# Hybrid decoder layer on one core: the attention sums are added tile by tile, and four other pieces of the order are moved

## The chip, the cores and the metric

The kernel runs on one core of a Trainium2 chip. Its time is the device time of one execution in microseconds (us), the median of several runs. TensorE (PE in the profile; PEld is its loading of weights) multiplies matrices, VectorE (DVE), ScalarE (ACT) and GpSimd (POOL) do the rest, and SyncE (SP) issues the DMA transfers. Each engine works through its own list of instructions in order and waits on semaphores that others count up.

## The reference, cut to what matters

The input x has 256 tokens of 2048 features, in float32.

```python
n = rmsnorm(h, attn_norm_w);  proj = n @ w_in            # 2048 -> 3376 columns
y_mla = mla_attention(...)                                # 8 heads of 128
y_nsa = nsa_attention(...)                                # 16 heads of 64, three branches, gated
y = concatenate([rmsnorm(y_mla, mla_out_norm_w), rmsnorm(y_nsa, nsa_out_norm_w)])
h = h + y @ w_o                                           # 2048 x 2048
n = rmsnorm(h, mlp_norm_w)
h = h + square(relu(n @ w_up)) @ w_down                   # 2048 -> 8192 -> 2048
return rmsnorm(h, final_norm_w)
```

## The kernel before, in words

The 256 tokens are two tiles of 128 (t = 0, 1). Each float32 product is made of three products in the type fp32r: the operand is split into a high part (`w_hi`, a copy by ScalarE) and a low part (`w_lo`, the difference, by VectorE), and TensorE multiplies high by high, high by low and low by high (L1266, L1267, L1270). All weights come as chunks of 1 MB at most, numbered c, through four buffers `raw` and two pairs `w_hi`, `w_lo`. So a chunk c can be split only when TensorE is done with chunk c - 2 (`w_used`), and TensorE starts it when `lo_done` has counted it.

Chunks 0 to 32 are the input projection, the MLA up projections and the compression weights. Chunk 22 is the first of the queries' weights; before it stand the copy of the values from PSUM (`v_sb`, L950, two tiles), the copy of the doubled keys (`k2h`, `k2l`) and chunk 21.

Chunks 33 to 48 are the output projection `y @ w_o`. Chunks 33 to 40 take the MLA half of y, 41 to 48 the NSA half, and in each half four chunks make the left 1024 output columns and four the right. A chunk has two blocks of 128 rows of weights and two tiles of tokens: four quarters of six matmuls with 512 columns. The sums of a group of four chunks stand in PSUM banks 0 and 1 (tile 0) and 2 and 3 (tile 1). After a group VectorE adds them, times the row factor `rm` or `rn` of that RMS norm, to the residual `h_sb` (`add_attention`, L1035, one instruction of 1024 columns for each tile), and the next group can't write the banks before.

A list, `PLAN`, written once and read by PE, ACT and DVE, sets the order up to chunk 44. In the output projection each quarter (`"q"`) is followed by one step (`"s"`) of attention: score, softmax, transposition and product with the values, spread over five steps (LAG = 3). `"hi"` and `"lo"` are the halves of the split of the next chunk. Step 51 finishes the last head, whose parts `yT` (L674, L832) chunk 44 needs; `"norm_n"` then sums the squares of the NSA half over the features (L1436). The root of the mean is taken by a guess from the bits on VectorE (`guess`, L851 and L852) and three rounds of Newton on GpSimd (`root_of_sums`, `improve`, L435 to L438).

Chunks 45 to 48 have no steps beside them. During them `h_sb` is turned (PE transposes, L1632, four 128-column blocks after chunk 46 and four after chunk 47) and copied out with the next norm's weights, split into high and low `xT` (`turned_hi`, L725, and `turned_lo`, L832). From chunk 49 on follows the MLP: the up projection of the first group (49 to 56), and a loop. `acc`, to which the down projection is added, is cleared by GpSimd (L518).

## Time and profile before

| | |
|---|---|
| median of 3 runs | 1080.29 us (1079.82 to 1081.09) |
| the profiled execution | 1080.06 us, of which 1078.0 us are its span |
| PE busy | 1058.9 us, 98% of the span |
| DVE, ACT, POOL busy | 634.5, 500.1, 101.7 us |
| granted clock of TensorE, mean | 0.998 |
| share of PE in the chain that ended last | 92% |

An engine's busy time is the time in which at least one of its instructions runs. Matmuls overlap, and their ends are modelled, so two matmuls' durations can't be summed. In a row of the timeline the first number is the start in us from the span's start, the second the duration of the row's instructions together, and square brackets give the idle time before them and who ended it.

### The profile page before, as it was taken

How to read it: one execution, taken by the hardware profiler on the slowest of the kernel's cores; microseconds unless marked ns; L12 is line 12 of the kernel's file. 1: busy time of each engine (PE TensorE's matmuls, PEld its weight loads, DVE VectorE, ACT ScalarE, POOL GpSimd, SP SyncE). 2: the span in 40 equal slices, each digit the busy share in tenths (PEclk: the TensorE clock that was granted, in tenths of full speed). 3: DMA queues.
4: the chain of work that ended last, by engine and by line, in shares of the span. 5: the costliest groups of instructions: out<-in, count | busy, mean ns of one | idle time of the engine just before them, and what ended most of it. 6: DMA issues, size and time to landing. Idle time of an engine off the chain costs nothing.

```text
span 1078.0 us, 14561 instructions
## 1 busy us (share of the span) xinstructions
PE 1058.9 (98%) x5706; PEld 906.8 (84%) x5706; DVE 634.5 (59%) x795; ACT 500.1 (46%) x620; POOL 101.7 (9%) x163
## 2 busy tenths in 40 slices
PE   8999999999999999999999999999999999999996
PEld 7889898888877888888888888888888888888885
DVE  4655765788765645556556545555655545655565
ACT  4646644776664544334334333433433433443434
POOL 2145100532203000000000000000000000000003
PEclk9999999999999999999999999999999999999999
DMA  9586562252335465655666656566666655656552
GB/s 332 165 209 198 180 211 85 73 196 78 94 103 157 157 195 179 191 182 192 192 195 195 188 187 186 183 192 192 195 194 189 189 183 185 191 192 195 194 196 78
DMA packets 89138, 190.44 MB, mean 177 GB/s; under 512 B 8758, under 2 KB 29836, under 8 KB 88716
## 3 DMA queue, kind: packets, MB, share of 16 engines
q1 hardware_dynamic: 88668, 189.41, 55.3%
q10 hardware_dynamic: 432, 0.52, 0.2%
q8 instruction: 24, 0.39, 0.1%
q14 instruction: 14, 0.11, 0.0%
HBM read 187.82 MB, written 2.10 MB: 176 GB/s over the span
## 4 chain that ended last, share of the span: by engine, by line
PE 92%; DVE 3%; ACT 2%; issue 1%; POOL 1%; DMA 0%; DVEq 0%; ACTq 0%
PE ps L1660 22%; PE ps L1266 14%; PE ps L1267 14%; PE ps L1270 14%; PE ps L1663 11%; PE ps L1533 2%; PE ps L1534 1%; PE ps L1537 1%; PE ps L1517 1%; PE ps L1492 1%; DVE w_lo L831 1%; PE ps L1331 1%; PE ps L1471 1%; PE ps L1518 1%; ACT w_hi L559 1%
## 5 line engine op out<-in xcount | busy, mean ns | idle before, releaser
L831 DVE TENSOR_TENSOR w_lo<-raw,w_hi 128x2048 fp32r<-128x2048 f32 (+4 forms) x198 | 402.6, 2036 | 354.7 <-ACT w_hi L566 287.8
L566 ACT ACTIVATE w_hi<-raw 128x2048 fp32r<-128x2048 f32 x119 | 228.1, 1917 | 396.3 <-PE ps L1270 200.8
L1660 PE MATMUL ps<-xT,w_hi 128*128 128x512 f32 x1024 | 279.5, 394 | 1.3 <-DVE h_sb L1035 1.0
L1660 PEld LDWEIGHTS ps<-xT,w_hi 128*128 128x128 f32 x1024 | 175.9, 189 | 26.1 <-issue 1.3
L1663 PEld LDWEIGHTS ps<-xT,w_lo 128*128 128x128 f32 x1024 | 157.1, 189 | 21.7
L1266 PE MATMUL ps<-w_hi,hidT 128*128 128x512 f32 x448 | 174.5, 390 | 0.0
L1267 PE MATMUL ps<-w_lo,hidT 128*128 128x512 f32 x448 | 174.4, 389 | 0.0
L1663 PE MATMUL ps<-xT,w_lo 128*128 128x256 f32 x1024 | 162.8, 281 | 0.0
L1270 PE MATMUL ps<-w_hi,hidT 128*128 128x512 f32 x448 | 138.1, 389 | 0.0
L559 ACT ACTIVATE w_hi<-raw 128x1024 fp32r<-128x1024 f32 (+3 forms) x75 | 103.8, 1391 | 72.0 <-PE ps L1270 41.4
L1270 PEld LDWEIGHTS ps<-w_hi,hidT 128*128 128x128 f32 x448 | 84.1, 188 | 17.6
L1267 PEld LDWEIGHTS ps<-w_lo,hidT 128*128 128x128 f32 x448 | 84.1, 188 | 17.2
L1266 PEld LDWEIGHTS ps<-w_hi,hidT 128*128 128x128 f32 x448 | 84.1, 188 | 17.1
L523 POOL TENSOR_TENSOR h_sb<-h_sb,fw 128x1024 f32<-128x1024 f32 x2 | 6.2, 3112 | 721.7 <-ACT sink L784 721.7
L1266 PE MATMUL ps<-w_hi,yT 128*128 128x512 f32 x128 | 54.4, 425 | 2.3 <-DVE h_sb L1035 2.3
L1267 PE MATMUL ps<-w_lo,yT 128*128 128x512 f32 x128 | 50.2, 392 | 0.0
L1266 PE MATMUL ps<-w_hi,xT 128*128 128x512 f32 x112 | 39.9, 356 | 0.4 <-DVE wcols L900 0.4
L1270 PE MATMUL ps<-w_hi,yT 128*128 128x512 f32 x128 | 39.8, 392 | 0.0
L1533 PE MATMUL ps<-xT,w_hi 128*128 128x256 f32 x128 | 37.1, 290 | 1.7 <-DVE w_lo L831 1.7
L1267 PE MATMUL ps<-w_lo,xT 128*128 128x512 f32 x112 | 37.9, 348 | 0.0
L662 ACT ACTIVATE probT<-ps 128x384 f32<-128x384 f32 (+1 forms) x48 | 22.2, 462 | 31.6 <-PE ps L1492 26.6
L1534 PE MATMUL ps<-xT,w_hi 128*128 128x256 f32 x128 | 36.2, 283 | 0.0
(309 smaller groups left out, 1309.1 us busy)
## 6 DMA issues: line engine op xcount, KB each, us to landing
raw<-in_w_up SPq DMA_DIRECT2D x64, 1024.0 KB, 5.3
raw<-in_w_down SPq DMA_DIRECT2D x64, 1024.0 KB, 5.5
raw<-in_w_o SPq DMA_DIRECT2D x16, 1024.0 KB, 5.6
raw<-in_w_in SPq DMA_DIRECT2D x8, 1024.0 KB, 5.2
raw<-in_w_in SPq DMA_DIRECT2D x8, 816.0 KB, 4.4
raw<-in_w_in SPq DMA_DIRECT2D x6, 832.0 KB, 8.2
raw<-in_mla_w_uq SPq DMA_DIRECT2D x12, 256.0 KB, 4.2
raw<-in_mla_w_ukv SPq DMA_DIRECT2D x4, 512.0 KB, 5.4
```

The lines of the kernel that those rows point to most:

```text
L559: act.activation(w_hi[:, split_slot(c), w0:w1], raw[:, raw_slot(c), w0:w1], ACT.Copy)\
L566: act.activation(w_hi[:, j % SPLIT, :], raw[:, j % RAW, :], ACT.Copy).then_inc(hi_done, 1)
L662: act.activation(probT[0:r, j % 2, 0:w], bank(6, w, 0, r), ACT.Copy).then_inc(pt_out, 1)
L831: return dve.tensor_tensor(dst, src, high.bitcast(F32), ALU.subtract)
L1266: pe.matmul(o, stationary(0, b, t), w_hi[:, slot, w], start=first, stop=False)
L1267: pe.matmul(o, stationary(0, b, t), w_lo[:, slot, w], start=False, stop=False)
L1270: m = pe.matmul(o, stationary(1, b, t), w_hi[:, slot, b * width + n0:b * width + n1], start=False, stop=last)
L1331: m = pe.matmul(flat[:, LOW[t] + n0:LOW[t] + n1], of_x(part, 2 * c + b, t), w_part[:, split_slot(c), CW * b + n0:CW * b + n1], start=c == ...
L1533: pe.matmul(o, w_hi[:, s, w], xT[:, 0, k, :], start=k == 0 and f == 0, stop=False)
L1534: m = pe.matmul(o, w_hi[:, s, w], xT[:, 1, k, :], start=False, stop=False)
L1660: pe.matmul(both, w_hi[:, slot, 512 * b + P * f:512 * b + P * f + P], xT[:, :, k0 + b, :], start=start and b == 0, stop=False)
L1663: m = pe.matmul(ps[:, b0 + f, 0:T], w_lo[:, slot, 512 * b + P * f:512 * b + P * f + P], xT[:, 0, k0 + b, :], start=False, stop=stop and b ...
```

## The change

Six edits, all of order or place, apart from the way the root for the NSA half is taken:

1. VectorE copies the 70 columns of `wcols` before it splits chunk 8, not after.
2. The second tile of the value copy (`v_sb`) moves behind the low halves of chunk 22, and the first low half of chunk 22 before the low part of the keys.
3. In the output projection the quarters go tile by tile: block 0 and block 1 of tile 0, then of tile 1. The add of a group is two entries, `("a", (n, t))`: tile 0 after the third quarter of the group's last chunk, tile 1 after the fourth. The attention steps that stood between groups now take the places behind quarters, so from chunk 37 each comes one quarter later than before, and from chunk 41 two. Chunks 45 to 48 are tile by tile as well.
4. The root for the NSA half: ScalarE loads the table of Sqrt and takes the root in `"norm_n"`, VectorE inverts it and does one round of Newton. GpSimd does nothing there. The table load that stood after chunk 49's split is gone.
5. The turned copies of blocks 4 to 7 stand after the split of chunk 49, behind the last group's add of tile 0. The transposes stay where they were.
6. `acc` is cleared once chunk 52 is split, not once the last head's low part is written.

```diff
-PLAN = [("hi", (CMP[0] + 1, 0)), ("k", "keys"), ("lo", (CMP[0] + 1, 0)), ("hi", (CMP[0] + 1, 1)), ("k", "rotary"), ("lo", (CMP[0] + 1, 1))]
+PLAN = [("hi", (CMP[0] + 1, 0)), ("lo", (CMP[0] + 1, 0)), ("k", "keys"), ("hi", (CMP[0] + 1, 1)), ("k", "rotary"), ("lo", (CMP[0] + 1, 1)),
+        ("k", "values")]
...
+ORDER = (((0, "hi", 0), (1, "lo", 0), (1, "hi", 1), (2, "lo", 1)), ((0, "hi", 0), (0, "lo", 0), (1, "hi", 1), (2, "lo", 1)))
 for _c in range(WO_M, WO_N + 4):
-    if _c in (WO_M + 4, WO_N):
-        PLAN += [("k", "add")] + _step(_s)
+    for _n, _part in enumerate((0, 2, 1, 3)):
+        PLAN += [("q", (_c, _part))]
+        if _n == 2 and (_c - WO_M) % 4 == 3:
+            PLAN += [("a", ((_c - WO_M) // 4, 0))]
+        PLAN += [(part, (_c + 1, half)) for at, part, half in ORDER[_c == WO_N + 3] if at == _n]
+        PLAN += _step(_s)
+        if _n == 3 and (_c - WO_M) % 4 == 3:
+            PLAN += [("a", ((_c - WO_M) // 4, 1))]
         _s += 1
...
+LATE = {WO_N + 5: TURNS[0], MLP0 - 1: TURNS[1]}
...
-            root_of_sums(1, rn[:, :])
-            pool.wait_ge(y_lo, 16)
+            pool.wait_ge(lo_done, MLP0 + 4)
             pool.memset(acc[:, :, :], 0.0).then_inc(acc0, 1)
...
+                elif i == "norm_n":
+                    act.activation(rc[:, 3:4], ones[:, :], ACT.Sqrt).then_inc(sqrt_table, 1)
+                    act.wait_ge(ysum_ok, 2)
+                    act.activation(rn[:, :], ssq[:, 8:10], ACT.Sqrt).then_inc(root_n, 1)
...
-            split_lo(8)
             dve.wait_ge(prm_t, 2)
             dve.tensor_copy(wcols[:, KT:NPRM], bank(4, NPRM - KT)).then_inc(wcols_ok, 1)
             dve.wait_ge(wcols_ok, 2)
+            split_lo(8)
...
-            for t in range(TT):
-                dve.tensor_copy(v_sb[:, t, :], flat[:, 2048 + 1024 * t:3072 + 1024 * t]).then_inc(v_out, 1)
+            dve.tensor_copy(v_sb[:, 0, :], flat[:, 2048:3072]).then_inc(v_out, 1)
...
-                guess(dst, square).then_inc(guessed, 1)
+                if part == 0:
+                    guess(dst, square).then_inc(guessed, 1)
+                    return
+                y, w, minus = dst, root_w[:, 0:TT], root_w[:, TT:2 * TT]
+                link(dve.tensor_scalar(minus, square, -0.5, None, ALU.mult))
+                dve.wait_ge(root_n, 1)
+                link(dve.reciprocal(y, y))
+                link(dve.tensor_tensor(w, y, y, ALU.mult))
+                link(dve.tensor_tensor(w, w, minus, ALU.mult))
+                dve.scalar_tensor_tensor(out=y, in0=w, scalar=1.5, in1=y, op0=ALU.add, op1=ALU.mult).then_inc(yr_ok, 1)
...
             for c in range(WO_N + 4, MLP0):
-                if c == WO_N + 4:
-                    add_attention(1, 0, 5, WO_N + 3)
                 split_lo(c + 1)
-                if WO_N + 5 <= c < MLP0 - 1:
-                    for k in TURNS[c - WO_N - 5]:
-                        turned_lo(k)
-            add_attention(1, 1, 6, MLP0 - 1)
+                if c == MLP0 - 1:
+                    add_attention(1, 1, 0, 6, MLP0 - 1)
+                for k in LATE.get(c, ()):
+                    turned_lo(k)
+            add_attention(1, 1, 1, 6, MLP0 - 1)
...
-                for b in range(blocks):
-                    for t in range(TT):
+                for outer in range(TT if by_tile else blocks):
+                    for inner in range(blocks if by_tile else TT):
+                        b, t = (inner, outer) if by_tile else (outer, inner)
```

What VectorE does between chunk 21's operand `blk` and the rows `rrow`, before. `w_lo` of 1024 columns is half a chunk, `k2l` the low part of the keys:

```order
L831 TENSOR_TENSOR blk<-blkf,blk 128x960
L950 COPY v_sb<-ps 128x1024 x2
L831 TENSOR_TENSOR k2l<-ps,k2h 128x512 x2
L831 TENSOR_TENSOR w_lo<-raw,w_hi 128x1024 x6
L1081 COPY rrow<-ps 128x256
```

And after the change:

```order
L837 TENSOR_TENSOR blk<-blkf,blk 128x960
L955 COPY v_sb<-ps 128x1024
L837 TENSOR_TENSOR w_lo<-raw,w_hi 128x1024
L837 TENSOR_TENSOR k2l<-ps,k2h 128x512 x2
L837 TENSOR_TENSOR w_lo<-raw,w_hi 128x1024
L1092 COPY v_sb<-ps 128x1024
L837 TENSOR_TENSOR w_lo<-raw,w_hi 128x1024 x4
L1095 COPY rrow<-ps 128x256
```

Ahead of the two halves of chunk 22 there is now one copy of the values, not two.

What VectorE does around the NSA norm, before, from the first low half of chunk 44's successor to the splits of chunks 46 and 47 (`ssq` is the mean square, `rn` the row factor):

```order
L831 TENSOR_TENSOR w_lo<-raw,w_hi 128x1024
L1021 TENSOR_SCALAR ssq<-ps 128x2
L851 TENSOR_SCALAR rn<-ssq 128x2
L852 TENSOR_SCALAR rn<-rn 128x2
L831 TENSOR_TENSOR w_lo<-raw,w_hi 128x1024 x3
L1035 SCALAR_TENSOR_TENSOR h_sb<-ps,rn,h_sb 128x1024 x2
L831 TENSOR_TENSOR w_lo<-raw,w_hi 128x2048 x2
```

And after the change:

```order
L837 TENSOR_TENSOR w_lo<-raw,w_hi 128x1024
L1026 TENSOR_SCALAR ssq<-ps 128x2
L1032 TENSOR_SCALAR root_w<-ssq 128x2
L1034 RECIPROCAL rn<-rn 128x2
L1035 TENSOR_TENSOR root_w<-rn 128x2
L1036 TENSOR_TENSOR root_w<-root_w 128x2
L1037 SCALAR_TENSOR_TENSOR rn<-root_w,rn 128x2
L1048 SCALAR_TENSOR_TENSOR h_sb<-ps,rn,h_sb 128x1024
L837 TENSOR_TENSOR w_lo<-raw,w_hi 128x1024
L1048 SCALAR_TENSOR_TENSOR h_sb<-ps,rn,h_sb 128x1024
L837 TENSOR_TENSOR w_lo<-raw,w_hi 128x2048 x2
```

The norm comes later against the splits, and one low half of chunk 45 now stands behind the root and the add of tile 0.

VectorE at the end of the output projection, before, from the splits of chunks 46 and 47 to that of chunk 50 (`xT` are the turned copies):

```order
L831 TENSOR_TENSOR w_lo<-raw,w_hi 128x2048 x2
L832 SCALAR_TENSOR_TENSOR xT<-ps,wcols,xT 128x256 x4
L831 TENSOR_TENSOR w_lo<-raw,w_hi 128x2048
L832 SCALAR_TENSOR_TENSOR xT<-ps,wcols,xT 128x256 x4
L831 TENSOR_TENSOR w_lo<-raw,w_hi 128x2048
L1035 SCALAR_TENSOR_TENSOR h_sb<-ps,rn,h_sb 128x1024 x2
L831 TENSOR_TENSOR w_lo<-raw,w_hi 128x2048
```

And after the change:

```order
L837 TENSOR_TENSOR w_lo<-raw,w_hi 128x2048 x2
L838 SCALAR_TENSOR_TENSOR xT<-ps,wcols,xT 128x256 x4
L837 TENSOR_TENSOR w_lo<-raw,w_hi 128x2048 x2
L1048 SCALAR_TENSOR_TENSOR h_sb<-ps,rn,h_sb 128x1024
L838 SCALAR_TENSOR_TENSOR xT<-ps,wcols,xT 128x256 x4
L1048 SCALAR_TENSOR_TENSOR h_sb<-ps,rn,h_sb 128x1024
L837 TENSOR_TENSOR w_lo<-raw,w_hi 128x2048
```

The second four turned copies moved from before the split of chunk 49 to between the two adds.

## Rows read from the trace of the kernel before

**Rows 1.** The page, part 1: busy time, share and instructions of each engine.

```profile
PE 1058.9 (98%) x5706; PEld 906.8 (84%) x5706; DVE 634.5 (59%) x795; ACT 500.1 (46%) x620; POOL 101.7 (9%) x163
```

**Rows 2.** Waits of PE, whole span: us in total, times, longest.

```profile
PE ps L1266 <- DVE h_sb L1035: 2.3, 3, 1.1
```

**Rows 3.** Timeline around the `wcols` copy: start, us, instruction, idle before.

```profile
49.36 0.22 DVE L900 COPY wcols<-ps 128x70 f32<-128x70 f32 x1
...
49.64 0.50 PE L1266 MATMUL ps<-w_hi,xT 128*128 128x512 f32 x1 [0.42 <-DVE wcols L900]
```

**Rows 4.** Timeline of DVE around the value copies.

```profile
117.02 2.35 DVE L950 COPY v_sb<-ps 128x1024 f32<-128x1024 f32 x2
119.28 1.28 DVE L831 TENSOR_TENSOR k2l<-ps,k2h 128x512 fp32r<-128x512 f32 x2
120.48 4.62 DVE L831 TENSOR_TENSOR w_lo<-raw,w_hi 128x1024 fp32r<-128x1024 f32 x4
```

**Rows 5.** Timeline of ACT there: the high part of chunk 22's second half.

```profile
118.40 1.06 ACT L559 ACTIVATE w_hi<-raw 128x1024 fp32r<-128x1024 f32 x1
```

**Rows 6.** Timeline of PE there: end of chunk 21, start of chunk 22.

```profile
120.98 0.28 PE L1563 MATMUL ps<-w_hi,blk 128*30 128x256 f32 x1
122.97 0.35 PE L1533 MATMUL ps<-xT,w_hi 128*128 128x256 f32 x1 [1.71 <-DVE w_lo L831]
```

**Rows 7.** Timeline where chunk 37 starts: last low half, last step, first matmul.

```profile
245.16 1.22 DVE L831 TENSOR_TENSOR w_lo<-raw,w_hi 128x1024 fp32r<-128x1024 f32 x1
...
250.15 0.38 PE L1518 MATMUL ps<-probT,vpad 128*128 128x128 f32 x2
251.66 0.47 PE L1266 MATMUL ps<-w_hi,yT 128*128 128x512 f32 x1 [1.12 <-DVE h_sb L1035]
```

**Rows 8.** Timeline of step 51, a quarter behind it, and the sum of squares.

```profile
322.10 0.69 PE L1504 MATMUL ps<-probT,vcmp 30*128 30x256 f32 x2
...
323.75 0.62 PE L1270 MATMUL ps<-w_hi,yT 128*128 128x512 f32 x2
324.92 0.61 PE L1436 MATMUL ps<-ones,sqacc 128*128 128x1 f32 x4 [0.55 <-POOL sqacc L485]
```

**Rows 9.** Timeline of ACT and DVE there: last head's copy, its low part, the mean.

```profile
322.83 0.38 ACT L672 ACTIVATE ysb<-ps 128x256 f32<-128x256 f32 x1 [1.33 <-PE ps L1504]
...
323.79 0.48 DVE L832 SCALAR_TENSOR_TENSOR yT<-ysb,wcols,yT 128x256 fp32r<-128x256 f32 x1 [6.95 <-ACT yT L674]
...
325.87 0.15 DVE L1021 TENSOR_SCALAR ssq<-ps 128x2 f32<-128x2 f32 x1
```

**Rows 10.** Timeline of PE: end of chunk 44, start of 45, turn after 46.

```profile
333.19 0.61 PE L1270 MATMUL ps<-w_hi,yT 128*128 128x512 f32 x2
334.23 0.47 PE L1266 MATMUL ps<-w_hi,yT 128*128 128x512 f32 x1 [0.43 <-DVE h_sb L1035]
...
345.24 1.03 PE L1632 MATMUL ps<-ident,h_sb 128*128 128x128 f32 x8
```

**Rows 11.** Timeline there: GpSimd clears `acc`, VectorE splits chunk 46.

```profile
332.70 3.52 POOL L518 MEMSET acc<- 128x4096 f32 x1
...
335.85 2.29 DVE L831 TENSOR_TENSOR w_lo<-raw,w_hi 128x2048 fp32r<-128x2048 f32 x1 [0.57 <-ACT w_hi L559]
```

**Rows 12.** Timeline of DVE at the end of the output projection.

```profile
352.51 1.66 DVE L832 SCALAR_TENSOR_TENSOR xT<-ps,wcols,xT 128x256 fp32r<-128x256 f32 x4 [1.15 <-ACT xT L725]
...
357.62 2.47 DVE L1035 SCALAR_TENSOR_TENSOR h_sb<-ps,rn,h_sb 128x1024 f32<-128x1024 f32 x2
```

**Rows 13.** Timeline of ACT there: the table load and the activation behind it.

```profile
355.39 1.28 ACT L745 ACT_TABLE_LOAD   x1
356.69 0.20 ACT L745 ACTIVATE rc<-ones 128x1 f32<-128x1 f32 x1
```

**Rows 14.** Timeline of PE there: end of chunk 48, start of chunk 49.

```profile
357.47 0.61 PE L1270 MATMUL ps<-w_hi,yT 128*128 128x512 f32 x2
359.04 1.17 PE L1660 MATMUL ps<-xT,w_hi 128*128 128x512 f32 x4 [0.95 <-DVE h_sb L1035]
```

More of the change, by code:

```diff
@@ L102, in _step @@
     if s > len(STEPS) + LAG:
-        return [("k", "norm_n")] if s == len(STEPS) + LAG + 1 else []
+        return [("k", "norm_n")] if s == len(STEPS) + LAG + 2 else []
     return [("s", s)] + ASIDE.get(s - NMLA, [])
+ORDER = (((0, "hi", 0), (1, "lo", 0), (1, "hi", 1), (2, "lo", 1)), ((0, "hi", 0), (0, "lo", 0), (1, "hi", 1), (2, "lo", 1)))
 for _c in range(WO_M, WO_N + 4):
-    if _c in (WO_M + 4, WO_N):
-        PLAN += [("k", "add")] + _step(_s)
-        _s += 1
-    for _n in range(4):
-        PLAN += [("q", (_c, _n))] + {0: [("hi", (_c + 1, 0))], 1: [("lo", (_c + 1, 0)), ("hi", (_c + 1, 1))],
-                                     2: [("lo", (_c + 1, 1))]}.get(_n, []) + _step(_s)
-        _s += 1
-assert _s > len(STEPS) + LAG + 1
+    for _n, _part in enumerate((0, 2, 1, 3)):
[6 more added lines that the diff above has]
+            PLAN += [("a", ((_c - WO_M) // 4, 1))]
+        _s += 1
+assert _s > len(STEPS) + LAG + 2
 HALVED = [i[0] for kind, i in PLAN if kind == "hi" and i[1] == 0]
@@ L743, in hidden_hi @@
                 act.activation(hidT[:, 0, 2 * pair:2 * pair + 2, :], hid[:, 2 * pair:2 * pair + 2, :], ACT.Copy).then_inc(hd_hi, 1)
-            act.activation(rc[:, 3:4], ones[:, :], ACT.Sqrt).then_inc(sqrt_table, 1)
             for c in range(MLP0 + 1, LOOP0):
@@ L1022, in mean_square, with add_attention @@
                 dve.wait_ge(ysum_ok, part + 1)
-                guess(dst, square).then_inc(guessed, 1)
-            def add_attention(part, n, group, last):
+                if part == 0:
[8 more added lines that the diff above has]
+                dve.scalar_tensor_tensor(out=y, in0=w, scalar=1.5, in1=y, op0=ALU.add, op1=ALU.mult).then_inc(yr_ok, 1)
+            def add_attention(part, n, t, group, last):
                 dve.wait_ge(yr_ok, part + 1)
@@ L1029, in add_attention @@
                 r = (rm, rn)[part]
-                for t in range(TT):
-                    sums_ready(dve, t, group, last)
-                    if part:
-                        dve.wait_ge(dve_free, 2 * n + t + 1)
-                    o = h_sb[:, t, 1024 * n:1024 * n + 1024]
-                    dve.scalar_tensor_tensor(out=o, in0=flat[:, 1024 * t:1024 * t + 1024], scalar=r[:, t:t + 1], in1=o,
-                                             op0=ALU.mult, op1=ALU.add).then_inc(dve_free, 1)
+                sums_ready(dve, t, group, last)
+                if part:
+                    dve.wait_ge(dve_free, 2 * n + t + 1)
+                o = h_sb[:, t, 1024 * n:1024 * n + 1024]
+                dve.scalar_tensor_tensor(out=o, in0=flat[:, 1024 * t:1024 * t + 1024], scalar=r[:, t:t + 1], in1=o,
+                                         op0=ALU.mult, op1=ALU.add).then_inc(dve_free, 1)
             def scale_queries(part):
@@ L1078, in _ @@
                     m.then_inc(k_ok, 1)
+                elif i == "values":
+                    dve.tensor_copy(v_sb[:, 1, :], flat[:, 3072:4096]).then_inc(v_out, 1)
                 elif i == "rows":
@@ L1093, in _ @@
                         low(high[other, e, :, :], full[r, :, :], high[r, e, :, :]).then_inc(q_lo, 1)
-                elif i == "add":
-                    add_attention(0, added_half, 3 + added_half, WO_M + 3 + 4 * added_half)
-                    added_half += 1
+                elif kind == "a":
+                    n, t = i
+                    add_attention(n // 2, n % 2, t, 3 + n, WO_M + 3 + 4 * n)
                 elif i == "norm_n":
@@ L1249, in _, with products @@
         def _(pe):
-            def products(slot, shape, stationary, base, start, stop, free=None, only=None, freed=False):
+            def products(slot, shape, stationary, base, start, stop, free=None, only=None, freed=False, by_tile=False):
                 blocks, width = shape
                 cols = [(n, min(width, n + 512)) for n in range(0, width, 512)]
-                for b in range(blocks):
-                    for t in range(TT):
+                for outer in range(TT if by_tile else blocks):
+                    for inner in range(blocks if by_tile else TT):
+                        b, t = (inner, outer) if by_tile else (outer, inner)
                         if only not in (None, TT * b + t):
@@ L1278, in _, with stream @@
             LOW, HIGH = (0, 1024), (2048, 3072)
-            def stream(c, tiles, k0, base, start, stop, free=None, only=None):
+            def stream(c, tiles, k0, base, start, stop, free=None, only=None, by_tile=False):
                 pe.wait_ge(lo_done, c + 1)
-                products(split_slot(c), chunk(c)[1], lambda part, b, t: tiles(part, k0 + b, t), base, start, stop, free, only, c in FREED)
+                products(split_slot(c), chunk(c)[1], lambda part, b, t: tiles(part, k0 + b, t), base, start, stop, free, only,
+                         c in FREED, by_tile)
             def of_x(part, k, t):
```

10 lines of the change are left out of this document (4 added, 6 removed).

## The prediction, made before the changed kernel ran

> **What bounds the kernel now.** I read the page's busy times first. PE is busy 98% of the span [rows 1], so the time is PE's work plus the moments in which PE stands still, and an edit that adds no matmul can only change those. Next come PE's waits by releaser: the dearest after the kernel's first microseconds is the add of the attention sums, three waits of 2.3 us together for the projection's own matmuls [rows 2], and a fourth, of 0.95 us, for the first matmul of the up projection [rows 14]. Then I looked for every bracket in PE's timeline. The change touches the places of seven: 0.42 us at chunk 8 [rows 3], 1.71 at chunk 22 [rows 6], 1.12 at chunk 37 [rows 7], 0.55 at the sum of squares [rows 8], 0.43 at chunk 45 [rows 10], 0.95 at chunk 49 [rows 14], and at chunk 41 what is left of the 2.3 us: 2.33 - 1.12 - 0.43 = 0.78. Behind chunk 49 PE leads every other engine and the change moves no order there, so what is saved ahead of it should reach the end.
>
> A wait costs a little more than its bracket. From chunk 45's first matmul to the transposes are 48 matmuls in 345.24 - 334.23 = 11.01 us: 0.229 each, 1.38 for a quarter, 5.50 for a chunk [rows 10]. The last two before a wait end, by the modelled end, 0.61 us after their start [rows 10, 14], where a stream would go on after 2 x 0.229 = 0.46. So each wait that goes gives back about 0.15 us more than its bracket.
>
> **Part by part.**
>
> The `wcols` copy. Both orders have the same two instructions, and PE needs both, the low part of chunk 8 and the columns. It starts 0.06 us after the copy's end at 49.58 [rows 3]; turned round, the split ends there instead. 0, at most 0.1 either way.
>
> The value copy. Two copies take 2.35 us, so one 1.18 [rows 4]. Before, the queue is two copies, two key parts, then the two low halves of chunk 22 at 1.16 each, the second of which ends at 120.48 + 2.31 = 122.8; PE starts 0.17 later [rows 4, 6]. Now one copy is out of it, so the half should end at 121.6. Its high part is ready at 118.40 + 1.06 = 119.5 [rows 5], no hindrance. PE could have gone on at about 121.1 [rows 6], so a wait of some 0.6 us stays and the whole copy counts: -1.18. The second copy now stands ahead of chunk 23's halves, where it stood ahead of them before, so those are no later than they were. Bounds -1.0 and -1.3.
>
> The adds before chunks 37 and 41. Tile 0's sums are complete after two quarters of the last chunk and are added during the third and fourth. With a step beside every quarter that is over 3 us of PE's time against 2.47 / 2 = 1.24 us for an add [rows 12]. Tile 1 is needed two quarters and steps into the next chunk. What the add is now ahead of: the second low half of the next chunk, which ended at 245.16 + 1.22 = 246.4 while the chunk, without its wait, would have started at about 250.4 [rows 7]; 1.24 us later is still nearly 3 us early. Behind that half is the scores' minimum of the step, whose product PE needs three steps later. Nothing is late next. Brackets 1.12 + 0.78 = 1.90, and 2 x 0.15.
>
> The sum of squares. It stands one quarter further from step 51 than before (two quarters, not one). The 0.55 is covered by 1.38: -0.55 - 0.15.
>
> What the later steps cost. Step 51 now stands before the last quarter but one ahead of chunk 44, so between its product and chunk 44 is a single quarter, and chunk 44's first matmul needs the last head's low part. The old trace shows the same stretch, with the sum where chunk 44 will be. The product starts at 322.10, ScalarE copies from 322.83, VectorE's low part ends at 323.79 + 0.48 = 324.27 [rows 8, 9]. From an add's end at 357.62 + 1.24 = 358.86 to PE's start at 359.04 is 0.18 [rows 12, 14], so PE can start at 324.45. Without the wait it would start at 323.75 + 0.46 = 324.21 [rows 8]. +0.24, a wait the old kernel doesn't have. Bounds 0 and 0.6.
>
> The root and chunk 45. I set chunk 44 at 324.45. Its first quarter ends at 325.83, the sums at about 326.4 (0.61 [rows 8]), the mean 0.15 later, 326.6 [rows 9]. ScalarE meanwhile makes the first high half from 324.3 to 325.4 (1.06 as in [rows 5]), loads the table (1.28) and runs the small activation (0.20) to 326.9 [rows 13]; the root itself, another 0.2, is done at 327.1. VectorE then has a reciprocal and three small instructions of about 0.17 with their own waits, to 328.0. Tile 0's sums are complete at 326.4 + 1.38 = 327.8. The add ends at 329.2, the second low half, whose high part was ready at 328.2, at 330.4, and PE may start at 330.55. PE is through chunk 44 at 327.8 + 2.76 = 330.56. So the wait of 0.43 goes, but the cover is nil: whatever makes this chain later comes back one for one. I take +0.1; bounds 0 and 0.8. Gone: -0.43 - 0.15.
>
> The end of the projection. Tile 0's sums are complete half a chunk, 2.75 us, before 357.93 (357.47 + 0.46 [rows 14]), at 355.2. In the old queue the low part of chunk 49 had ended by 357.7, since the adds start at 357.62 [rows 12]. Now the four turned copies, 1.66 us on VectorE [rows 12], no longer stand ahead of it, so it ends at about 356.1, tile 0's add at 357.3, before PE wants it. The copies end at 359.0, tile 1's add at 360.3. PE needs that one only for the third of four column groups, at 357.93 + 2.75 = 360.7. -0.95 - 0.15, with 0.2 us to spare on the second add. Bounds: all of it, or half.
>
> The clearing of `acc` takes 3.52 us [rows 11]. Its reader is ScalarE's copy after chunk 52, an up chunk of the same column count as 5.50 us of the projection. It starts when chunk 52 is split, so before PE starts it, and is done with 2 us to spare. Beside it VectorE splits chunk 53. In the old trace it ran beside VectorE's adds and met the start of a split that took 2.29 us [rows 11]. 0, bound 1 us if it held up a split for its whole overlap. The Trainium skill, page "SBUF — State Buffer", section "Reading the diagram", states that a VectorE instruction with two SBUF inputs contends only with a GpSimd one that reads SBUF. A clearing reads nothing, so by that rule it is free as well.
>
> **The sum.** Gone: 1.18 + (1.12 + 0.78 + 0.55 + 0.43 + 0.95 = 3.83) + 5 x 0.15 = 5.76. New: 0.24 + 0.1 = 0.34. Net -5.42. The profiled execution took 1080.06 us (1078.0 of span, 2.06 around it), so 1074.6; the runs' median is 0.23 above that execution: 1074.9.
>
> **The rivals.**
>
> A. The root's chain is late. ScalarE's table load is now on the way to `rn`, and with no cover at chunk 45 a delay of one more load's length, 1.28 us, is a wait of 1.3. For it: the count above ends level with PE. Against: in the trace the next activation starts 0.02 us after the load's end [rows 13], and nothing else is queued on ScalarE between the two halves. If it comes, 1074.9 + 1.3 = 1076.2. The Trainium skill ("ScalarE: Activation LUTs", section "What ACT_TABLE_LOAD costs") prices a switch at the load plus a drain of about 1.38 us. By that rule this rival is what happens, 1076.2; the row just named shows no such drain behind the load.
>
> B. Only the plain moves pay, and the steps' new places give the adds' gain back. The score pipeline runs one and two quarters later against halves and adds; if VectorE is late for a step wherever an add stands, the 1.90 + 0.30 of chunks 37 and 41 is lost and A's wait too: 1074.9 + 2.2 + 1.3 = 1078.4, still 1.9 faster, which is within what can't be told from no change.
>
> C. Slower. VectorE's queue turns into the bound of the eight chunks 37 to 44: the second low half of each now stands behind heavier steps, and PE waits for `lo_done` at each chunk. It decides once halves that are ready 4.0 us early (250.4 - 246.4 [rows 7]) are more than 4 us later; from there on each chunk costs its excess, and it takes over 5.42 / 8 = 0.7 us in each to be slower. With 1 us in each: 1074.9 + 8 = 1082.9. Against it: VectorE's instructions are the same in number, but for two small ones, and it is busy 59% of the span [rows 1].
>
> **How the numbers follow.** My forecast 0.76; A 0.14; B 0.07; C 0.03. A measurement of this kernel can tell about 0.2% from no change, 2.2 us, so below 1078.1 is faster, above 1082.4 slower. All of the forecast and A, and none of B's centre but its better side, are faster: 0.76 + 0.14 + 0.02 = 0.92. Same 0.05, slower 0.03. The range: at its best the new waits are nil and the copy gives 1.3: 1074.9 - 0.5; a further 0.6 for brackets that were worth more than I gave them: 1073.8. At its worst all upper bounds of the forecast (0.36 + 0.7 + 0.5 for half of the last wait, + 0.1) come near A's 1076.2 plus some of its own spread: 1077.0.
>
> **What would show it.** In the new profile: PE's matmul of chunk 22 starts about 1.2 us earlier with a bracket of about 0.5. No bracket of an add on L1266 or on the up projection's first matmul. The sum of squares without a bracket; a new one of some 0.2 us on chunk 44's first matmul, from VectorE's low part of y. A bracket of 0 to 0.3 at chunk 45. ACT_TABLE_LOAD between two halves, with the root within 0.3 us of the mean. The last matmul of chunk 48 about 5 us earlier than before, and the loop shifted by the same. I am wrong if PE waits for `probT` or `w_lo` in chunks 37 to 44, if the table load is followed by a gap over 1 us, or if the shift at chunk 49 is not found at the end.

## The result, and the profile after

The changed kernel takes 1073.97 us (median of 4 runs, 1073.28 to 1074.28) against 1080.29: a ratio of 0.994, 95% interval 0.9924 to 0.9955. The forecast was 1074.9 with a range of 1073.8 to 1077.0. Its profiled execution took 1074.28 us, 1072.5 of them span; the old one had 1078.0 [rows 1], so the span is 5.5 us shorter, where the sum had 5.42.

The page's busy times, to be held against [rows 1]. PE is busy 0.9 us less with the same 5706 instructions, near the 0.75 us that the sum gave for the lost overlap of five waits. GpSimd has lost its root, and VectorE has three instructions more:

```profile
PE 1058.0 (99%) x5706; PEld 906.8 (85%) x5706; DVE 635.0 (59%) x798; ACT 500.8 (47%) x621; POOL 96.4 (9%) x150
```

The waits of PE by releaser, without those of the first microseconds (us in total, times, longest). No `h_sb` is left, where [rows 2] had 2.3 us. The two waits for `probT` stand at 205.85 and 209.17, ahead of chunk 37; the old kernel has the same two:

```profile
PE ps L1280 <- DVE w_lo L837: 0.6, 1, 0.6
PE ps L1548 <- DVE w_lo L837: 0.5, 1, 0.5
PE ps L1507 <- ACT probT L666: 0.4, 2, 0.2
```

The timeline of PE at seven places: the first matmuls of chunks 8, 22, 37, 44, 45 and 49 and, last, one in the MLP that waits for a split in both kernels, a late point that no edit touches:

```profile
49.95 0.47 PE L1280 MATMUL ps<-w_hi,xT 128*128 128x512 f32 x1 [0.64 <-DVE w_lo L837]
...
121.96 0.35 PE L1548 MATMUL ps<-xT,w_hi 128*128 128x256 f32 x1 [0.54 <-DVE w_lo L837]
...
247.97 0.48 PE L1280 MATMUL ps<-w_hi,yT 128*128 128x512 f32 x1
...
323.69 0.50 PE L1280 MATMUL ps<-w_hi,yT 128*128 128x512 f32 x1
...
329.85 0.50 PE L1280 MATMUL ps<-w_hi,yT 128*128 128x512 f32 x1
...
353.58 1.07 PE L1675 MATMUL ps<-xT,w_hi 128*128 128x512 f32 x4
...
406.24 1.21 PE L1675 MATMUL ps<-xT,w_hi 128*128 128x512 f32 x4 [0.30 <-DVE w_lo L837]
```

Against [rows 3, 6, 10, 14] these starts differ by +0.31 at chunk 8, -1.01 at chunk 22, -4.38 at chunk 45 and -5.46 at chunk 49. Chunks 37 and 44 can't be compared in this way, since steps have moved across their starts. The late point stood at 411.81 before: -5.57. What was won up to chunk 49 is what arrives.

VectorE at the root for the NSA half: the mean, the add of tile 0 and the low half that PE waits for:

```profile
326.06 0.15 DVE L1026 TENSOR_SCALAR ssq<-ps 128x2 f32<-128x2 f32 x1
...
327.38 1.28 DVE L1048 SCALAR_TENSOR_TENSOR h_sb<-ps,rn,h_sb 128x1024 f32<-128x1024 f32 x1
328.58 1.22 DVE L837 TENSOR_TENSOR w_lo<-raw,w_hi 128x1024 fp32r<-128x1024 f32 x1
```

and ScalarE there:

```profile
324.91 1.28 ACT L715 ACT_TABLE_LOAD   x1
326.20 0.20 ACT L715 ACTIVATE rc<-ones 128x1 f32<-128x1 f32 x1
326.31 0.19 ACT L717 ACTIVATE rn<-ssq 128x2 f32<-128x2 f32 x1
```

The low half ends at 328.58 + 1.22 = 329.80 and chunk 45 starts at 329.85: VectorE's chain and PE arrive together, as the count said. Behind the table load (it ends at 326.19) the small activation starts 0.01 us later.

### The profile page after: what moved, and what is told of

The parts are those of the page before. It is cut to its first block, busy times and chain, and to the rows that moved or that the text cites. A ratio compares the mean times of both kernels' runs of the same rounds, so it can differ in the third digit from the quotient of the medians.

```text
span 1072.5 us, 14557 instructions
## 1 busy us (share of the span) xinstructions
PE 1058.0 (99%) x5706; PEld 906.8 (85%) x5706; DVE 635.0 (59%) x798; ACT 500.8 (47%) x621; POOL 96.4 (9%) x150
## 4 chain that ended last, share of the span: by engine, by line
PE 95%; DVE 2%; ACT 2%; issue 1%; DMA 0%; DVEq 0%; ACTq 0%
PE ps L1675 22%; PE ps L1280 15%; PE ps L1281 15%; PE ps L1284 15%; PE ps L1678 11%; PE ps L1548 2%; PE ps L1532 2%; PE ps L1549 1%; PE ps L1552 1%; PE ps L1507 1%; PE ps L1346 1%; DVE w_lo L837 1%; PE ps L1486 1%; PE ps L1533 1%; PE ps L1485 1%; PE ps L1490 1%
```

## The experiments

Runs of one kernel differ by half a microsecond and more, and a part of that lies ahead of everything that is changed here: in the profiled executions PE's first wait for the DMA of x was 1.3 to 2.0 us long, and chunk 8 started anywhere between 49.04 and 49.98 in ten kernels that are the same up to there. So each effect is also read in the trace: the start of the late point (406.24) less that of chunk 8 (49.95), 356.29 in the changed kernel. "Shift" below is the difference from that; each is read from one profiled execution. Where edit 1 lies between, the last two matmuls of chunk 7 take chunk 8's place (48.78 after, 48.69 before). From there the old kernel's late point is at 411.81 - 48.69 = 363.12 and the changed one's at 357.46: the change is worth 5.66 us by this measure. On the chips of these runs the kernel before took 1079.57 to 1079.79.

### The third edit, undone in three ways

**u_adds**: both adds behind the last step.

```diff
-        if _n == 2 and (_c - WO_M) % 4 == 3:
-            PLAN += [("a", ((_c - WO_M) // 4, 0))]
...
-            PLAN += [("a", ((_c - WO_M) // 4, 1))]
+            PLAN += [("a", ((_c - WO_M) // 4, 0)), ("a", ((_c - WO_M) // 4, 1))]
```

> The changed kernel, quarters still tile by tile, but in the entries of chunks 36, 40 and 44 both adds stand behind the last quarter and its step, not tile 0's behind the third quarter. My theory (the place of tile 0's add is what removed the waits): in the changed kernel VectorE reaches that place at 250.02, so tile 0's add ends at 251.28 and PE, which started chunk 37 at 247.97, starts it at about 251.46: a wait of some 3.4 us and 0.15 of lost overlap, the same again at chunk 41, and about 0.2 at chunk 45, where the low half goes first. About +7.3 us: 1081.3. Rival (the order of the quarters is what pays, and the place of the add is of little weight): at most the old brackets of chunks 37 and 41 come back, 1.90 + 0.30: 1076.2 or less.

Measured 1078.36, ratio 0.9991 (0.9981 to 1.0001); shift +5.04. Its timeline, VectorE's two adds and PE's first matmuls of chunks 37 and 41:

```profile
248.54 2.46 DVE L1046 SCALAR_TENSOR_TENSOR h_sb<-ps,rm,h_sb 128x1024 f32<-128x1024 f32 x2
...
249.95 0.47 PE L1278 MATMUL ps<-w_hi,yT 128*128 128x512 f32 x1 [2.46 <-DVE h_sb L1046]
...
297.13 0.47 PE L1278 MATMUL ps<-w_hi,yT 128*128 128x512 f32 x1 [2.01 <-DVE h_sb L1046]
```

The waits are at the places and of the kind expected, and 0.9 and 1.4 us shorter. At chunk 37 that is because VectorE comes to the adds at 248.54, 0.8 us earlier, counted from chunk 8, than in the trace from which I took it, where an add of 1.28 us stood ahead. The two waits, with 0.15 of lost overlap each, are 4.77 of the 5.04 us; the rival's 2.2 is excluded.

**u_blocks**: quarters block by block, adds where they are.

```diff
-    for _n, _part in enumerate((0, 2, 1, 3)):
+    for _n, _part in enumerate((0, 1, 2, 3)):
...
-... t + 1), by_tile=True)
+... t + 1), by_tile=False)
```

> The changed kernel with the quarters block by block again (block 0 of both tiles, then block 1), adds still one per tile at their new places. My theory (place of the adds pays, not the order of the quarters): tile 0's sums are complete after the third quarter, still before VectorE reaches the add at 244.2, so no wait at chunks 37 and 41. At chunk 45 the sums come a quarter later: third quarter's end about 328.0, add to 329.3, low half to 330.5, PE at 330.6, not 329.85: +0.7. At chunk 49 the add can start about 352.4 and ends at 353.7: +0.2. Together +0.9: 1074.9. Rival (tile by tile gives the gain): the brackets of chunks 37 and 41 come back as well, 1.12 + 0.78 + 0.30 more: 1077.1.

Measured 1076.28, ratio 0.9974 (0.9962 to 0.9985); shift +3.01, by the timeline of PE in four waits (at the second quarters of chunks 37 and 41, not the first, and at the starts of chunks 45 and 49):

```profile
250.53 0.48 PE L1280 MATMUL ps<-w_hi,yT 128*128 128x512 f32 x1 [0.50 <-DVE h_sb L1048]
...
296.12 0.47 PE L1280 MATMUL ps<-w_hi,yT 128*128 128x512 f32 x1 [0.30 <-DVE h_sb L1048]
...
331.47 0.50 PE L1280 MATMUL ps<-w_hi,yT 128*128 128x512 f32 x1 [1.32 <-DVE w_lo L837]
...
355.63 1.16 PE L1675 MATMUL ps<-xT,w_hi 128*128 128x512 f32 x4 [0.28 <-DVE h_sb L1048]
```

The 0.7 and 0.2 us that I gave chunks 45 and 49 were brackets of 1.32 and 0.28, and chunks 37 and 41 do wait, by 0.50 and 0.30, not by the rival's 1.12 and 0.78. At chunks 37 and 41 tile 0's add is in time, as I said. But block by block the second quarter is already tile 1's, so the last add has one quarter of cover and not two. At chunk 45 tile 0's sums come a quarter later, and the add waits 1.41 us for them. Undone alone, the order of the quarters costs 3.0 us and the place of tile 0's adds 5.0.

**u_steps**: steps between the groups again, sums and norm one or two quarters earlier.

```diff
+    if _c in (WO_M + 4, WO_N):
+        PLAN += _step(_s)
+        _s += 1
```

> The changed kernel with tile by tile quarters and one add per tile, but the attention steps between the groups at their old places, so that all steps behind chunk 37 come one quarter earlier and those behind chunk 41 two, with the sum of squares and the norm. My theory (their new places cost the 0.12 us lost at chunk 44's start and the 0.10 at chunk 45, nothing more; the adds' gain comes from the adds' own places): no bracket of an add at chunks 37 and 41, one of up to 0.5 at the sum of squares, total within 0.3 of the changed kernel, 1073.7 to 1074.2. Rival (the steps' new places are what gives VectorE the time for the adds): brackets of about 1.1 and 0.8 at chunks 37 and 41 come back, +2.2, 1076.2.

Measured 1075.95, ratio 0.9967 (0.9955 to 0.998); shift +2.02. PE's timeline has no bracket of an add, but four others:

```profile
253.60 0.55 PE L1510 MATMUL ps<-ident,prob 128*128 128x128 f32 x3 [0.17 <-ACT probT L669]
256.92 0.55 PE L1510 MATMUL ps<-ident,prob 128*128 128x128 f32 x3 [0.23 <-ACT probT L669]
...
321.84 0.61 PE L1454 MATMUL ps<-ones,sqacc 128*128 128x1 f32 x4 [0.54 <-POOL sqacc L493]
...
325.68 0.47 PE L1283 MATMUL ps<-w_hi,yT 128*128 128x512 f32 x1 [0.36 <-DVE w_lo L840]
```

1.30 us of brackets and some 0.15 to 0.2 of lost overlap for each. My +-0.3 fell; the rival's size came out, by other waits than it named. Both `probT` waits come where ScalarE makes a high half first (252.13 to 253.18 ahead of the first); why it is too late here and not in the changed kernel is open. The sum of squares waits as in [rows 8]. And VectorE, which must finish the root first, waits 0.50 us for ScalarE's part of it and comes to the second low half of chunk 44 only at 324.31. So the later steps are a part of the gain. The prediction booked 0.70 us for the sum of squares and 0.24 against; undone, with the norm moved along, they cost 2.02.

### The other edits, each undone alone

**u_values**: both value copies ahead of chunk 22.

```diff
-PLAN = [("hi", (CMP[0] + 1, 0)), ("lo", (CMP[0] + 1, 0)), ("k", "keys"), ... ("lo", (CMP[0] + 1, 1)),
-        ("k", "values")]
+PLAN = [("hi", (CMP[0] + 1, 0)), ("k", "keys"), ("lo", (CMP[0] + 1, 0)), ... ("lo", (CMP[0] + 1, 1))]
...
-            dve.tensor_copy(v_sb[:, 0, :], flat[:, 2048:3072]).then_inc(v_out, 1)
+            for t in range(TT):
+                dve.tensor_copy(v_sb[:, t, :], flat[:, 2048 + 1024 * t:3072 + 1024 * t]).then_inc(v_out, 1)
```

> The changed kernel with both value copies ahead of the low halves of chunk 22, as before. My theory: PE's start of chunk 22 comes 1.1 us later (bracket 1.7, not 0.54), nothing behind it takes the wait up, and the end is 1.1 later: 1075.1. Rival (the next chunks absorb it, as chunk 11 did with the 0.22 us of chunk 8): bracket of 1.7 at chunk 22, but the anchor of chunk 37 moves by less than 0.3: 1074.0 to 1074.3.

Measured 1075.39, ratio 0.9962 (0.9948 to 0.9976); shift +1.17. The first matmul of chunk 22:

```profile
123.11 0.36 PE L1548 MATMUL ps<-xT,w_hi 128*128 128x256 f32 x1 [1.67 <-DVE w_lo L836]
```

1.12 us later than in the changed kernel, counted from chunk 8, and as much at the end: nothing behind it takes up a delay.

**u_root**: the root by `guess` and GpSimd, the table load behind the projection.

```diff
-                if part == 0:
-                    guess(dst, square).then_inc(guessed, 1)
-                    return
...
+                guess(dst, square).then_inc(guessed, 1)
...
+            root_of_sums(1, rn[:, :])
             pool.wait_ge(lo_done, MLP0 + 4)
```

> The changed kernel with the root for the NSA half taken as before: the guess on VectorE, three rounds of Newton on GpSimd, no table load in the norm (it is back behind the projection). My theory (the root edit is what the later steps are paid with): the GpSimd chain took 6.3 us from the mean in the old kernel, so from 326.06 the factor is there at 332.4, tile 0's add ends at 333.7, the low half behind it at 334.9, and PE starts chunk 45 at 335.0, not 329.85: +5.2, so 1079.2, nearly all that the change won. Rival (the root's engine is free, since the old kernel's chain was hidden as well): +0.5 at most, 1074.5. Rival A of the forecast (the table load delays the chain): its removal would give something back elsewhere, under 1074.0.

Measured 1078.38, ratio 0.9985 (0.9976 to 0.9995), runs from 1076.02 to 1079.9; shift +2.82. The timeline: GpSimd's first and last instruction of the root, VectorE's add, PE's chunk 45:

```profile
326.32 0.20 POOL L440 TENSOR_TENSOR root_w<-rn 128x2 f32<-128x2 f32 x1 [2.47 <-DVE rn L856]
...
329.61 0.18 POOL L495 COPY root_w<-rn 128x2 f32<-128x2 f32 x1
...
329.83 1.28 DVE L1037 SCALAR_TENSOR_TENSOR h_sb<-ps,rn,h_sb 128x1024 f32<-128x1024 f32 x1 [3.59 <-POOL root_w L495]
...
332.30 0.50 PE L1269 MATMUL ps<-w_hi,yT 128*128 128x512 f32 x1 [2.77 <-DVE w_lo L835]
```

Direction and place were right, the size half. GpSimd's rounds took 3.5 us here and 6.3 in the old kernel. The old timeline shows why: the first of these instructions met a split on VectorE and took 1.10 us, the second took 0.20, and two later ones met splits again and took 1.22 and 1.06:

```profile
326.33 1.22 DVE L831 TENSOR_TENSOR w_lo<-raw,w_hi 128x1024 fp32r<-128x1024 f32 x1
...
326.50 1.10 POOL L435 TENSOR_TENSOR root_w<-rn 128x2 f32<-128x2 f32 x1 [1.64 <-DVE rn L852]
327.68 0.20 POOL L436 TENSOR_TENSOR root_w<-root_w,ssq 128x2 f32<-128x2 f32 x1
```

A GpSimd instruction of 0.20 us that met a VectorE split lasted until the split ended (327.60 and 327.55).

**two_tables**: two further table loads ahead of the root, a doubled cost and not an undone edit.

```diff
                     act.activation(rc[:, 3:4], ones[:, :], ACT.Sqrt).then_inc(sqrt_table, 1)
+                    act.wait_ge(sqrt_table, 1)
+                    act.activation(rc[:, 3:4], ones[:, :], ACT.Exp).then_inc(sqrt_table, 1)
+                    act.wait_ge(sqrt_table, 2)
+                    act.activation(rc[:, 3:4], ones[:, :], ACT.Sqrt).then_inc(sqrt_table, 1)
```

> The changed kernel with two more table loads (Exp, then Sqrt again, each with a small activation) in the norm on ScalarE, ahead of the root. My theory (the root's chain bounds chunk 45, cover is nil, the price is one for one and a load costs 1.28 and its small activation about 0.2): the root comes 2.97 us later, at 329.3 instead of 326.31, and PE starts chunk 45 at 332.8, not 329.85: +2.9, 1076.9. Rival A (a load also waits for a drain of 1.38 us): each further load costs 2.7 us, chunk 45 5.5 us later, 1079.4. Rival (there is cover at chunk 45 that the count did not see): +1.9 or less, 1075.9.

Measured 1077.91, ratio 0.9986 (0.9976 to 0.9995), runs from 1076.38 to 1079.67; shift +2.97. ScalarE's loads, the root, and PE's chunk 45:

```profile
324.24 1.28 ACT L715 ACT_TABLE_LOAD   x1
...
325.76 1.28 ACT L717 ACT_TABLE_LOAD   x1
...
328.68 0.19 ACT L721 ACTIVATE rn<-ssq 128x2 f32<-128x2 f32 x1
...
332.22 0.50 PE L1284 MATMUL ps<-w_hi,yT 128*128 128x512 f32 x1 [2.96 <-DVE w_lo L841]
```

3.00 us on ScalarE, 3.00 at chunk 45, 2.97 at the late point: one for one. A switch costs 1.28 us and its small activation. The Trainium skill ("ScalarE: Activation LUTs", section "What ACT_TABLE_LOAD costs") adds a drain of about 1.38 us to each switch, 2.66 us together; by that the two further ones would have cost 5.3 us and their activations, an estimate from the page's figure. This trace does not agree: the three loads and the small activations follow one another within 0.02 us.

**u_late**: the turned copies of blocks 4 to 7 before the split of chunk 49.

```diff
-LATE = {WO_N + 5: TURNS[0], MLP0 - 1: TURNS[1]}
+LATE = {WO_N + 5: TURNS[0], WO_N + 6: TURNS[1]}
```

> The changed kernel with the turned copies of blocks 4 to 7 before the split of chunk 49, as before. My theory (they stood in the way of the last adds): ScalarE's four copies put its high part of chunk 49 from 347.5 to about 349.1, so VectorE's low part of it runs from 351.1 to 353.3, not 349.44 to 351.73, tile 0's add to 354.5, and PE starts chunk 49 at 354.7 instead of 353.58, with a bracket of about 1.0 from the add: +1.1, 1075.1 (by the ratio to the changed kernel). Rival (tile by tile alone had covered the last add, since tile 0's sums are now complete half a chunk early): no bracket at chunk 49, +0.

Measured 1075.22, ratio 0.9958 (0.9944 to 0.9973); shift +1.19. ScalarE's high part of chunk 49, and PE's start of that chunk with the old kernel's bracket:

```profile
348.90 1.94 ACT L563 ACTIVATE w_hi<-raw 128x2048 fp32r<-128x2048 f32 x1
...
354.50 1.16 PE L1675 MATMUL ps<-xT,w_hi 128*128 128x512 f32 x4 [0.95 <-DVE h_sb L1048]
```

Tile by tile alone does not remove this wait. The copies' new place does, or rather that of ScalarE's part of them: with it ahead, the high part of chunk 49 starts at 348.90 and not at 347.50, and the adds at 353.08 and not at 351.65.

**u_clear**: `acc` cleared behind the last head's low part.

```diff
-            pool.wait_ge(lo_done, MLP0 + 4)
+            pool.wait_ge(y_lo, 16)
```

> The changed kernel with acc cleared as soon as the last head's low part is written (323.6), so for 3.5 us beside the low half, the mean and the root's small instructions on VectorE. My theory (a clearing beside VectorE costs it nothing): chunk 45 starts where it does in the changed kernel, within 0.1 us, no VectorE instruction longer, 1074.0. Rival (the two engines take turns at SBUF): VectorE's low half of 1.22 us or the root's small instructions take up to twice as long or start later, and chunk 45, which has no cover, starts up to 1 us later: 1075.0.

Measured 1075.5, ratio 0.996 (0.9944 to 0.9975); shift +1.13. GpSimd's clearing, a split and a small instruction of the root on VectorE, and PE's chunk 45:

```profile
323.86 3.54 POOL L522 MEMSET acc<- 128x4096 f32 x1
...
324.63 1.22 DVE L837 TENSOR_TENSOR w_lo<-raw,w_hi 128x1024 fp32r<-128x1024 f32 x1 [1.30 <-ACT w_hi L563]
...
325.96 1.47 DVE L1032 TENSOR_SCALAR root_w<-ssq 128x2 f32<-128x2 f32 x1
...
330.72 0.50 PE L1280 MATMUL ps<-w_hi,yT 128*128 128x512 f32 x1 [1.10 <-DVE w_lo L837]
```

My theory fell. The split of 1.22 us beside the clearing takes no longer than elsewhere, and neither does the mean, which reads PSUM (0.15 us from 325.77). But a `tensor_scalar` of two elements, from SBUF to SBUF, takes 1.47 us instead of 0.17 and ends at 327.43, when the clearing ends (327.40). So the sixth edit is no neutral one in the new kernel: the short root stands where the clearing ran, and chunk 45 has no cover.

**u_wcols**: the columns behind the split of chunk 8.

```diff
+            split_lo(8)
             dve.wait_ge(prm_t, 2)
...
-            split_lo(8)
```

> The changed kernel with the 70 columns of wcols copied behind the split of chunk 8, as before. My theory, from the two traces: PE starts chunk 8 0.2 us earlier (bracket 0.42, not 0.64), and loses it again by chunk 11, whose own wait is set by another chain; end 0 to 0.1 different. Rival (the edit costs what its bracket says): 0.2 less at the end. The time of the runs can hardly tell; the trace's later starts do.

Measured 1074.06, ratio 0.9948 (0.9931 to 0.9964). PE's starts of chunks 8 and 10:

```profile
49.87 0.51 PE L1280 MATMUL ps<-w_hi,xT 128*128 128x512 f32 x1 [0.42 <-DVE wcols L906]
...
59.05 0.50 PE L1280 MATMUL ps<-w_hi,xT 128*128 128x512 f32 x1
```

Its chunk 7 ends 0.14 later than in the changed kernel. Less that, chunk 8 starts 0.22 earlier, the chunk at 59.05 at the same 58.91, the late point 0.07 earlier. The edit costs 0.22 us and has it back two chunks on. That chunk is called 11 in what was expected, but it is chunk 10: VectorE splits chunk 8 at 47.94, chunk 9 at 51.01, and the next at 56.98, just ahead of it. What sets its start is seen in the changed kernel, on ScalarE and VectorE:

```profile
55.39 1.55 ACT L563 ACTIVATE w_hi<-raw 128x1632 fp32r<-128x1632 f32 x1
...
56.98 1.88 DVE L837 TENSOR_TENSOR w_lo<-raw,w_hi 128x1632 fp32r<-128x1632 f32 x1 [0.68 <-ACT w_hi L563]
```

The low part ends at 58.86 and PE starts at 58.91. VectorE was idle for 2.65 and 0.68 us before it. It waits for ScalarE, whose work begins when PE has finished chunk 7 (the high part of chunk 9, two copies, the sums of squares, then the high part of chunk 10) and in either order of VectorE's two instructions reaches that high part 6.61 us after the last matmuls of chunk 7 started.

### The third edit alone

**e3_alone**: the diffs of u_values, u_root, u_late, u_clear and u_wcols taken together, so that of the change only the third edit is left.

> The kernel before with the third edit alone: tile by tile quarters, one add per tile, the steps at their later places. The other five are undone (root by GpSimd too). Theory (the parts are not additive, the steps' later places have to be paid with the short root): against the kernel before, chunks 37 and 41 give 2.2, the sum of squares 0.7, chunk 44 takes 0.1, and chunk 45 takes 2.9 where it took 0.6, as it did with the old root in the changed kernel: net about -0.4, 1079.2, with brackets of 1.7 at chunk 22 and about 1 at chunk 49. Rival (each part brings its own term, as my sum had it): 2.9 less the 0.24 of chunk 44, 1076.9 or so.

Measured 1080.05, ratio 1.0001 (0.9991 to 1.001). Counted from chunk 8 (0.19 earlier than the old one's), chunk 45 is 0.48 us ahead of the old kernel, as expected. Then the clock fell in the profiled execution. Its PE timeline (two matmuls of chunk 45), and its stretches from 333 us (us; busy time and count of PE, PEld, DVE, ACT, POOL; granted clock; DMA share; GB/s):

```profile
333.56 0.50 PE L1269 MATMUL ps<-w_hi,yT 128*128 128x512 f32 x1 [2.77 <-DVE w_lo L834]
...
335.11 0.63 PE L1269 MATMUL ps<-w_hi,yT 128*128 128x512 f32 x1
```

```profile
333.00:336.00 3.00, 2.44 (x9) 1.94 (x10) 3.00 (x3) 0.00 (x0) 1.51 (x1) 0.83 0.44 89
336.00:339.00 3.00, 3.00 (x10) 2.39 (x9) 0.90 (x1) 0.00 (x0) 0.00 (x0) 0.60 1.01 312
```

From about 335 to 338.4 us matmuls stood 0.43 us apart instead of 0.23, the lower of the engine's two levels, 1.2 GHz; from 339 us on the granted clock is 1.00 again. From chunk 45 to 49 it took 26.45 us, the old kernel 24.81, so 1.64 were lost, and the late point is 1.15 us behind instead of 0.49 ahead. By the trace, with that loss taken out, the third edit alone brings half a microsecond; by the times it brings nothing that can be told (1080.05 against 1079.79). Even its shortest execution, 1079.05, excludes the additive rival's 1076.9.

### Two that go further

**half22**: PE starts chunk 22 on its first low half.

```diff
+                elif c == A_IN[0]:
+                    m.then_inc(half_lo, 1)
...
+                first = c == A_IN[0]
+                if first:
+                    pe.wait_ge(half_lo, 1)
...
+                    if first and quarter == 2:
+                        pe.wait_ge(lo_done, c + 1)
```

> The changed kernel with one more semaphore: PE starts chunk 22 once its first low half is there, and waits for the second only before its third quarter. My theory: the wait of 0.54 us is for the second low half alone (ready at 121.82), the first was ready at 119.5, so PE goes on at about 121.4 instead of 121.96 and finds the second half ready: -0.55, and the end moves by the same, as it did for the value copy: 1073.4. Rival (what is saved there is regained further on, as at chunk 11): bracket gone, end unchanged.

**v_best**: the same, and `wcols` copied by ScalarE.

```diff
-            dve.tensor_copy(wcols[:, KT:NPRM], bank(4, NPRM - KT)).then_inc(wcols_ok, 1)
...
+            act.activation(wcols[:, KT:NPRM], bank(4, NPRM - KT), ACT.Copy).then_inc(wcols_ok, 1)
```

> half22 and beside it wcols copied from PSUM by ScalarE, so that VectorE has only the split ahead of chunk 8. My theory: chunk 8's bracket shrinks by about 0.2, which is lost again by chunk 11, as with the old order, so the same end as half22: 1073.4. Rival (ScalarE's copy is late, or delays the high part of chunk 9): up to 0.5 more than half22. It should beat the kernel before by 0.6%.

half22 took 1072.6 us, ratio 0.9934 (0.9919 to 0.9949), shift -0.80; v_best 1072.62, ratio 0.9933 (0.9919 to 0.9946), shift -1.30 (counted from the last matmuls of chunk 7, at 47.85, since an edit lies between). Chunk 22 in half22; then, in v_best, chunk 8, ScalarE's high part of chunk 10, and chunk 10:

```profile
120.32 0.28 PE L1556 MATMUL ps<-xT,w_hi 128*128 128x256 f32 x1
```

```profile
48.75 0.47 PE L1282 MATMUL ps<-w_hi,xT 128*128 128x512 f32 x1 [0.37 <-DVE w_lo L839]
...
54.15 1.55 ACT L563 ACTIVATE w_hi<-raw 128x1632 fp32r<-128x1632 f32 x1
...
57.69 0.47 PE L1282 MATMUL ps<-w_hi,xT 128*128 128x512 f32 x1
```

The bracket of chunk 22 is gone. Counted from chunk 8 it starts 0.73 us earlier, the bracket and its lost overlap, and that arrives at the end; I had expected 0.55. In v_best, counted from the end of chunk 7, chunk 8 starts 0.26 us earlier than in half22, and chunk 10 is still 0.29 ahead, where I had expected nothing. It is ahead because ScalarE reaches the high part of chunk 10 0.32 us sooner, 6.30 us after the end of chunk 7 instead of 6.62: an idle time of 0.42 us between its sums of squares in half22 is not there in v_best. Why it is gone is not shown; that VectorE had one copy less to do is not the reason, since VectorE is idle ahead of both its splits. Another 0.2 us is won in small steps up to about chunk 37, with no bracket that says where. Both kernels are faster than the one before. Against the changed kernel their intervals overlap in the times; only the traces order the three.

## Why the prediction was right

The mechanism and the sum held: net -5.42 forecast, -5.5 of span found. That the total is met within 0.1 us is partly luck: the start lost 0.11 and the value copy gave 0.06 less than forecast, while chunks 37 to 44 gave 0.24 more. The point lies 0.9 us above the median. 0.3 of that is a term that the sum had at nothing: the new execution has 1.78 us around its span, not 2.06. It goes with the root: 60 executions of the kernels with the new root have 1.74 to 1.87 us there, while u_root has 2.00 in the median, e3_alone 1.99 and the kernel before 2.01 to 2.06. Why is not shown. The rest is scatter from run to run: u_wcols, whose late point is that of the changed kernel within 0.07 us, took 5.5 us less than the kernel before on its chip, not 6.3.

- **Value copy**: -1.18 forecast. From +0.11 at chunk 21 to -1.01 at chunk 22 is -1.12, and undone it costs 1.17.
- **`wcols`**: 0 to 0.1 forecast. 0.22 at chunk 8, nothing at the end. Right at the end, too small at the place. It does not arrive because the start of chunk 10 hangs on ScalarE's chain, and not because it is small.
- **Chunks 37 and 41, the sum of squares, chunk 44's new wait**: from the quarter ahead of chunk 37 (-0.99) to the end of chunk 44 (-3.89) the gain is 2.90; the terms were 2.20, 0.70 and +0.24, together 2.66. The new wait was over-estimated: chunk 44 starts 0.58 us after the last two matmuls of its forerunner, which is 0.12 lost and not 0.24, and leaves no bracket. The other 0.12 can't be put to one term.
- **Chunk 45**: -0.58 + 0.1 = -0.48 forecast, -4.38 + 3.89 = -0.49 found. "The cover is nil, one for one" was tested by itself and holds to 0.03 us.
- **Chunk 49**: -1.10 forecast, -1.12 found (-4.34 to -5.46), by the mechanism named (u_late).
- **Rival A** (drain or late root) is excluded by the after trace and by two_tables. **B** and **C** did not come: no bracket for `probT` or `w_lo` in chunks 37 to 44.

What was wrong lies in the reasons, not in the sum.

The cover of chunk 37: I wrote that the second low half, an add later, would still be nearly 3 us early. It ends at 246.62 and PE starts the chunk at 247.97, so 1.35 us are left. I had set the add against the old start at 250.4, but a step of 1.3 us that stood ahead of the chunk now stands behind its first quarter. For the same reason rival C's threshold of 4 us was too wide. And VectorE has three instructions more, not two.

The step on the clearing: I wrote that it costs nothing since it reads nothing. That is so where it stands now, from 371.83 to 375.35, beside a split that keeps its 2.29 us. The Trainium skill, "SBUF — State Buffer", section "Reading the diagram", names two kinds of VectorE instruction, one with two SBUF inputs, which contends only with a reading GpSimd, and one in a mode that takes both ports, which contends with any. I used the first half. The runs agree with both: the split beside the clearing kept its 1.22 us in u_clear, the `tensor_scalar` lasted until its end, and GpSimd's reading instructions lasted until the ends of splits.

The terms as separate gains: each was read as a bracket of its own. The runs make another account, from the old kernel on. The third edit alone is worth 0.49 without the fallen clock. With it in place the root brings 2.82, the turned copies 1.19, the value copy 1.17: 5.67, where 5.66 were found (so close by luck, since each is read from one execution; the root is undone with the late clearing in place, which is taken to be free beside the old root). The third edit undone in part costs 2.0, 3.0 or 5.0. So its brackets of [rows 7] pay only as far as the root is short, since the later steps push the norm against chunk 45, and the clearing's place is worth 1.1 only because the root is where it is.

## What to carry to other kernels

Where the bound engine is never short of work but for brackets, undo each edit alone in the new kernel: the parts of a change can't be priced one by one by old brackets, even where their sum comes out, because one part spends the cover that another makes. Before moving a chain of tiny instructions, look which large instruction of VectorE or GpSimd will run beside it, since a 0.2 us instruction can last as long as its neighbour. And before a small delay is priced, follow the chain that sets the next start: if it does not pass through the place that is moved, as at chunk 10, the delay does not arrive.
